# A hybrid layer in another order: z chunks inside the attention rounds, inverted blocks placed by ScalarE

## The reference

```python
qa_l, ka_l, va_l, za_l, g_l, be_l, qb_l, kb_l, vb_l = split_hybrid_projection(a_lat @ w_in, conv_w, ...)
qa_c, ka_c, va_c, za_c, g_c, be_c, qb_c, kb_c, vb_c = split_hybrid_projection(a_ctx @ w_in, conv_w, ...)
o_ctx_a, s_fwd, s_bwd = bidirectional_delta(qa_c, ka_c, va_c, g_c, be_c, zeros, zeros, ctx_out)
o_lat_a, _, _ = bidirectional_delta(qa_l, ka_l, va_l, g_l, be_l, s_fwd, s_bwd, True)
qb_l = apply_axial_rope(qb_l, cos, sin)
kb_l = apply_axial_rope(kb_l, cos, sin)
o_lat_b = latent_attention_blocks(group(qb_l), k_all, v_all)
y = rms_norm(o_lat_a, out_norm) * silu(za_l)
y_lat = concatenate([y, o_lat_b]) @ w_out
```

## Time and profile before

| what | us |
|---|---|
| median of three executions | 2290.75 (2288.51 to 2290.96) |
| the profiled execution, its own time | 2290.72 |
| its span, first to last instruction | 2288.9 |
| TensorE matmul busy | 2220.6 |
| VectorE busy | 1618.4 |
| ScalarE busy | 1156.7 |
| GpSimd busy | 153.3 |

### The profile page before, as it was taken

The page is one execution under the profiler, slowest core; times in us unless marked ns, Lnnn a source line. Parts: engine busy times, 40 slices in busy tenths (PEclk is TensorE's granted clock), DMA queues, the critical chain, the costliest instruction groups (busy, mean ns, idle before and its releaser), DMA issues.

```text
span 2288.9 us, 41418 instructions
## 1 busy us (share of the span) xinstructions
PE 2220.6 (97%) x17332; PEld 2045.3 (89%) x17332; DVE 1618.4 (71%) x2749; ACT 1156.7 (51%) x1937; POOL 153.3 (7%) x142
## 2 busy tenths in 40 slices
PE   7999999999989999999999999999999999999998
PEld 3665889998879999999999989997779999999998
DVE  4399668655977645798557687577988557799654
ACT  3425445443365446756346564345556345957343
POOL 0013000000000000000000000015630000000000
PEclk9999999999999999999999999999999999999999
DMA  8148054555244554415554325562025554514552
GB/s 346 73 183 317 37 221 166 185 186 201 92 166 168 187 186 171 173 57 184 184 182 157 141 93 203 184 221 74 19 94 183 184 184 169 183 55 166 185 184 92
DMA packets 50873, 368.46 MB, mean 161 GB/s; under 512 B 5632, under 2 KB 5888, under 8 KB 6528
## 3 DMA queue, kind: packets, MB, share of 16 engines
q1 hardware_dynamic: 50544, 363.72, 43.2%
q10 hardware_dynamic: 144, 2.10, 0.2%
HBM read 364.75 MB, written 1.05 MB: 160 GB/s over the span
## 4 chain that ended last, share of the span: by engine, by line
PE 81%; DVE 11%; ACT 5%; issue 2%; DMA 0%; SPq 0%; DVEq 0%; POOL 0%; ACTq 0%
PE psum L263 67%; DVE weight_rest L257 2%; PE psum L4508 1%; PE psum L3069 1%; PE psum L4509 1%; ACT weight_parts L221 1%; PE psum L4530 1%; PE psum L3703 1%; PE psum L2719 1%; DVE work L2021 1%; PE psum L4544 1%; DVE work L3533 1%; DVE spare L2509 0%; DVE work L2508 0%; DMA weight_ring<-stream_dram 0%
## 5 line engine op out<-in xcount | busy, mean ns | idle before, releaser
L263 PE MATMUL psum<-input_parts,weight_parts 128*128 128x256 f32 x5184 | 933.0, 283 | 6.0 <-DVE work L1489 1.8
L263 PEld LDWEIGHTS psum<-input_parts,weight_parts 128*128 128x128 f32 x5184 | 801.0, 189 | 11.2 <-issue 5.3
L263 PE MATMUL psum<-input_parts,weight_rest 128*128 128x256 f32 x2592 | 733.6, 283 | 0.0
L257 DVE TENSOR_TENSOR weight_rest<-weight_ring,weight_parts 128x1024 fp32r<-128x1024 f32 x528 | 621.1, 1222 | 151.8 <-ACT weight_parts L221 151.3
L221 ACT ACTIVATE weight_parts<-weight_ring 128x1024 fp32r<-128x1024 f32 x540 | 538.1, 1051 | 128.2 <-PE psum L263 105.6
L263 PEld LDWEIGHTS psum<-input_parts,weight_rest 128*128 128x128 f32 x2592 | 488.9, 189 | 0.0
L263 PE MATMUL psum<-hidden_parts,weight_parts 128*128 128x256 f32 x2496 | 450.7, 283 | 2.6 <-DVE weight_rest L257 1.3
L263 PEld LDWEIGHTS psum<-hidden_parts,weight_parts 128*128 128x128 f32 x2496 | 385.1, 189 | 6.0 <-issue 3.4
L263 PE MATMUL psum<-hidden_parts,weight_rest 128*128 128x256 f32 x1248 | 352.2, 282 | 0.0
L263 PEld LDWEIGHTS psum<-hidden_parts,weight_rest 128*128 128x128 f32 x1248 | 235.0, 188 | 0.0
L1473 ACT ACTIVATE work<-psum 128x256 f32<-128x256 f32 x118 | 45.3, 384 | 352.3 <-PE psum L263 349.9
(11 more groups left out here) (532 smaller groups left out, 2855.4 us busy)
## 6 DMA issues: line engine op xcount, KB each, us to landing
weight_ring<-stream_dram SPq DMA_DIRECT2D x340, 1024.0 KB, 4.8
constants<-constants_dram SPq DMA_DIRECT2D x1, 2304.0 KB, 12.5
work<-s_bc_dram ACTq DMA_DIRECT2D x1, 2048.0 KB, 9.8
work<-ctx_dram SPq DMA_DIRECT2D x1, 1024.0 KB, 5.5
residual<-x_dram SPq DMA_DIRECT2D x1, 1024.0 KB, 7.6
work<-first_dram SPq DMA_DIRECT2D x1, 1024.0 KB, 14.9
out_dram<-residual SPq DMA_DIRECT2D x4, 256.0 KB, 2.1
vectors<-vectors_dram SPq DMA_DIRECT2D x1, 486.5 KB, 11.8
```

Source lines behind the costliest of these rows:

```text
L257: ins = dve.tensor_tensor(self.rest[:, i % RING, cols], self.ring[:, i % RING, cols], self.parts[:, s % SPLITS, cols].bitcast(F32), ALU.su ...
L263: mm = pe.matmul(*args, **kw)
```

## The change

The diff puts the projection into another order: the delta q heads come right behind the k heads, then two v heads, then k, v and q of attention, then the last two v heads. The four z chunks leave the projection: one each is computed in attention rounds 0, 1, 4 and 5, half of it in each of the round's two places for a fill; ScalarE takes them plainly, and one silu over all four stands in the delta stage. Fills stay in rounds 2, 3, 6 and 7, and the projection has sixteen slabs of them instead of eight. VectorE's list of the projection is written anew for this, with three takings inside it. ScalarE gathers the diagonal blocks (`collect`) and puts the inverted ones into their matrices (`place`, in rounds 4 to 7), where GpSimd did; GpSimd keeps the clearing. The attention's probabilities get memory of their own, since their place now still holds the layer's input for z. The core of the diff:

```diff
+        self.attention_work = sb("attention_work", [P, 8 * T2])
...
-FILL_AFTER = (11, 13, 15, 17)
-BESIDE_PROJECTION = 2 * len(FILL_AFTER)
+FILL_AFTER = {9: 2, 11: 2, 13: 4, 15: 4, 17: 4}
+BESIDE_PROJECTION = sum(FILL_AFTER.values())
+LATE_CHUNKS = 4
+LATE_ROUNDS = (0, 1, 4, 5)
+FILL_ROUNDS = (2, 3, 6, 7)
...
-        self.sums_after = {4: (0, 1), 5: (2,), 6: (3, 4), 7: (5, 6), 8: (7,), 9: (8,)}
-        self.lower_after = {8: 0, 9: 1, 11: 2, 13: 3}
+        self.sums_after = {4: (0, 1), 5: (2,), 6: (3,), 11: (4,), 13: (5,), 14: (6,), 15: (7,), 16: (8,)}
+        self.lower_after = {8: 0, 9: 1, 10: 2, 11: 3}
+        self.turns_after = {16: 4, 17: 1}
...
+    def late_silu(self, act):
+
+        act.wait_ge(*self.late_taken[-1])
+        z = self.k.area(H_Z, LATE_CHUNKS * T)
+        act.activation(z, z, ACT.Silu).then_inc(self.late_ready[0], 1)
...
+        self.lower.vector(dve, 2)
+        self.normalize(dve, 4)
+        k.background.take(dve, STRIPS)
+        self.lower.vector(dve, 3)
+        self.normalize(dve, 5)
+        self.blocks.gather(dve)
+        self.normalize(dve, 6)
+        self.blocks.steps(dve, 0, 8)
+        self.normalize(dve, 7)
+        k.background.take(dve, 2 * STRIPS)
+        self.blocks.steps(dve, 8, 15)
+        self.normalize(dve, 8)
+        self.convolve(dve, 10)
+        k.background.take(dve, 3 * STRIPS)
         dve.wait_ge(k.consts_loaded, 16)
         for i in range(5):
             self.rotate(dve, i)
...
         self.convolve(dve, 11)
         self.blocks.steps(dve, 15, EARLY_STEPS)
-        k.background.take(dve, BESIDE_PROJECTION)
...
+            if r in LATE_ROUNDS:
+                self.late_jobs[r] = k.job(k.hyb.late_taken[LATE_ROUNDS.index(r)])
             if r >= 3 and r % 2 == 1:
...
+    def beside(self, pe, r, half):
+
+        if r in LATE_ROUNDS:
+            self.k.hyb.late_half(pe, LATE_ROUNDS.index(r), self.late_jobs[r], half)
+        else:
+            self.k.background.fill(pe, 2)
...
+            if r - 1 in LATE_ROUNDS:
+                k.hyb.take_late(act, LATE_ROUNDS.index(r - 1), self.late_jobs[r - 1])
...
+            if r in (4, 5):
+                self.blocks.place(act, r - 4, 0)
+            if r in (6, 7):
+                self.blocks.place(act, r - 6, 1)
...
-                k.background.take(dve, BESIDE_PROJECTION + 2 * r + 2)
+                k.background.take(dve, BESIDE_PROJECTION + 2 * sum(n < r for n in FILL_ROUNDS))
...
+        k.background.take(dve, BEFORE_DELTA)
...
+                far = self.lc[at, :, :].rearrange("p r (s m) -> p s m r", s=SEQS)
+                for s in range(SEQS):
+                    ins = act.activation(self.b[at, s, :, at], far[:, s], ACT.Identity)
+            else:
+                ins = act.activation(self.a[at, :, at], self.near[at, :, :].rearrange("p s m -> p m s"), ACT.Identity)
```

More of the change, by code:

```diff
@@ L1787, in tensor @@
         front = k.front
+        turned = 0
         for n, (job, (_, tokens, _)) in enumerate(zip(self.jobs, self.chunks)):
@@ L1890, in scalar @@
             else:
-                act.activation(x, job.ap[:, 0:seqs * T], ACT.Silu if kind == "silu" else ACT.Identity)\
-                   .then_inc(self.taken[n][0], 1)
+                act.activation(x, job.ap[:, 0:seqs * T], ACT.Identity).then_inc(self.taken[n][0], 1)
             if 1 <= n <= 4:
                 self.silu(act, n - 1)
-            if n >= 18:
-                self.silu(act, 2 * n - 32)
-                self.silu(act, 2 * n - 31)
             if n == 4:
@@ L1912, in scalar @@
                     self.lower.take_turned(act, m - 1)
-            if n == 14:
+            if n == 13:
                 self.lower.take_turned(act, 3)
+                self.blocks.collect(act)
+            if n == 16:
+                self.lower.tails(act)
+                act.preload_act_table_set("silu_and_others")
+                for i in range(4, 10):
+                    self.silu(act, i)
+        self.silu(act, 10)
+        self.silu(act, 11)
         act.preload_act_table_set(EXP_LN)
@@ L1984, in vector @@
             self.rotate(dve, i)
-        self.convolve(dve, 7)
-        k.background.take(dve, STRIPS)
-        self.lower.vector(dve, 3)
-        for i in range(8, 10):
-            self.convolve(dve, i)
-        self.blocks.gather(dve)
-        self.blocks.steps(dve, 0, 8)
-        self.convolve(dve, 10)
-        self.blocks.steps(dve, 8, 15)
         self.convolve(dve, 11)
         self.blocks.steps(dve, 15, EARLY_STEPS)
-        k.background.take(dve, BESIDE_PROJECTION)
     def gate_values(self, dve):
@@ L2030, in normalize @@
         if 4 <= i < 9:
-            gain = self.k.v("hyb_q_norm" if i < 8 else "hyb_k_norm")
+            gain = self.k.v("hyb_q_norm" if i > 4 else "hyb_k_norm")
         else:
@@ L2113, in tensor @@
                               start=True, stop=True).then_inc(job.full[0], 1)
-                k.background.fill(pe, 2)
+                self.beside(pe, r, 0)
             if r >= 3 and r % 2 == 1:
@@ L2450, in gpsimd @@
             at = self.quarter(q)
[L2451 to L2474 removed]
+            ins = act.activation(self.near[at, :, :], l[at, :, at], ACT.Identity)
+        ins.then_inc(self.gathered[0], 1)
     def quarter(self, q):
@@ L2855, in vector @@
             if first < len(self.steps) - DIRS:
-                k.background.take(dve, BESIDE_PROJECTION + 2 * len(k.attention_rounds) + first + 2)
+                k.background.take(dve, BEFORE_DELTA + first + 2)
         k.weights.split_through(dve, self.next_slab)
@@ L4823, in hyb_columns @@
 def hyb_columns():
-    return np.r_[512:1024, 2064 + hyb_heads(), 2576:2832, 0:512, 1024:2048]
+    return np.r_[512:1024, 0:512, 1024:1280, 2576:2832, 2064 + hyb_heads(), 1280:2048]
 def beside_projection(w, mod):
+    early = len(w) - LATE_CHUNKS // 2
     out, n = [], 0
-    for j in range(len(w)):
+    for j in range(early):
         if j:
             out.append(w[j:j + 1])
-        if 2 * j + 1 in FILL_AFTER:
+        fills = FILL_AFTER.get(2 * j + 1, 0)
+        out.append(mod[n:n + fills])
+        n += fills
+    for r in range(2 * B_PAIRS):
+        if r in FILL_ROUNDS:
             out.append(mod[n:n + 2])
             n += 2
+        elif LATE_ROUNDS.index(r) % 2 == 0:
+            j = early + LATE_ROUNDS.index(r) // 2
+            out.append(w[j:j + 1])
     return np.concatenate(out + [mod[n:]], 0)
```

153 lines of the change are left out of this document (83 added, 70 removed).

## The result

| | before | after |
|---|---|---|
| median, us | 2289.63 (2288.03 to 2290.96, 4 executions) | 2315.37 (2309.49 to 2321.79, 4 executions) |
| ratio | 1 | 1.0113 (95% interval 1.0085 to 1.0142) |
| profiled execution, us | 2290.72 | 2321.79 |
| span, us | 2288.9 | 2320.0 |
| first product of the delta stage | 233.23 | 256.08 |

Slower by 25.7 us, as to sign what was forecast (+14.7), as to size above the range's end of 2311. The profiled execution is the longest of the four; its extra 31.1 us of span fall into 22.85 up to the delta stage, 6.8 from there to a mark 296 us further on (the first table load of ScalarE after 500 us, 529.46 before, 559.09 now) and 1.5 behind that.

What follows compares the result with a forecast made beforehand. TensorE, 97% busy, bounds the kernel, so its waits were summed: 3.7 + 0.9 + 6.0 + 2.6 + 1.1 + clock 1.7 - (0.99 and 0.53) + 0.2 = +14.7 us on 2290.75: 2305.4, range 2297 to 2311.

Steps and rivals of the forecast that it cites:

- wait A: Fill after chunk 15 in the projection: TensorE waits for VectorE's second taking of modulation rows, 3.7 us.
- rotation 4: Before the first attention scores: TensorE waits for VectorE's rotation after head 8 is turned, 0.9 us.
- wait B: Rounds 0 and 1: TensorE waits for first probabilities, behind VectorE's convolution 11 and inversion steps 15 to 22, 6.0 us.
- wait C: Round 2: the second score job waits for probabilities 2 because of its PSUM bank, 2.6 us.
- D, E, F, H: Smaller waits: z-job banks in rounds 1 and 6, output 0's copy, the delta stage's first mask; 5.95 us charged.
- G: End of the attention rounds: the last values product waits for ScalarE's copy, 0.9 us.
- half clock behind A: After the fill's wait behind chunk 15: one fall of the granted clock to 0.50, charged at 1.7 us.
- weight ring: Weight slabs on SP's queue: the same megabytes in another order, so nothing charged.
- the gates: The gates' wait near 80 us, longer because one head's sum left from before it, 0.2 us.
- The rule on GpSimd and VectorE: GpSimd reading SBUF blocks VectorE instructions with two SBUF inputs; 2.1 us handed back to VectorE, not subtracted from the forecast.
- third rival: ScalarE's strided block copies at GpSimd's price, 7.4 us on top: 2309 or 2313; sign: over 1.5 us each; chance 0.08.
- anything behind the delta stage: All behind the delta stage keeps its length; a changed length there would mean something unnamed is at work.

Runs made afterwards that it cites:

- second taking: Changed kernel with VectorE's second taking of modulation rows ahead of inversion steps 0 to 7 instead of behind them: 2311.4 us, ratio 1.0089.
- steps early: Changed kernel with inversion steps 15 to 22 moved from behind convolution 11 to ahead of normalization 8: 2306.9 us, ratio 1.0082.
- five products: Changed kernel with five 128 x 512 products that nobody reads put on TensorE ahead of round 0's turning: 2313.6 us, ratio 1.0111.
- two at a time: Changed kernel with two modulation slabs behind every odd chunk from 5 to 15, and the first two takings earlier: 2302.3 us, ratio 1.0052.
- The three mends: Changed kernel with placing back on GpSimd, two slabs behind odd chunks 5 to 15, and inversion steps 15 to 22 ahead of normalization 8: 2294.0 us, ratio 1.0023.

## Why the prediction was wrong

By its terms, up to the first product of the delta stage in the profiled execution (the pauses of before that fall away, 7.3 us, are the same on both sides):

| term | charged | measured |
|---|---|---|
| wait A | 3.7 | 4.00 |
| rotation 4 | 0.9 | 0.94 |
| wait B | 6.0 | 5.52 |
| wait C, with the half clock ahead of it | 2.6 | 1.30 + 1.86 |
| D, E, F, H | 5.95 | 1.22 + 1.53 + 1.25 + 1.85 = 5.85 |
| G, values behind ScalarE | 0.9 | 1.32 + 2.58 = 3.90 |
| half clock behind A | 1.7 | 5.35 - 3.66 = 1.69 |
| weight ring | 0 | 2.07 + 0.38 = 2.45 |
| half clock behind the ring | 0 | 5.38 - 3.62 = 1.76 |
| half clock at the last values | 0 | 2.97 - 1.95 = 1.02 |
| the gates | 0.2 | 1.87 - 1.74 = 0.13 |

Charged, less 7.3: 14.7. Measured, less 7.3: 23.1, where the trace has 22.85; its projection started 0.28 us earlier than before (43.64 for 43.92), which is the difference.

**What was right.** A, the rotation, B and the sums D to H but for G are within half a microsecond of what was laid end to end from the rows of before; undoing A's and B's causes (second taking, steps) took these waits away, and brought out 1.50 us more at the ring and 1.53 more at C behind them. C itself was nearly right at full clock: 2.83 with the steps early and with five products. "Behind wait B a fall costs nothing" is shown by the five products. That the delta stage's silu and its table loads cost nothing holds: "to mark" is 296.22 with them and 296.23 before. The rule on GpSimd and VectorE stays out of the sum: convolution 10's four operations take 3.11 us now, as the rows without GpSimd said (3.05).

**Step 1 that failed: "ScalarE gets them for nothing as long as its pauses in the rounds hold them".** Two errors in one. The price was read off a row of contiguous elements, 9 us in all, though the only row with this access pattern, GpSimd's, said 16.4; the copies took 16.25, those of 1024 elements 1.98 each, over the 1.5 that was named as the third rival's sign. And a pause that holds the work does not hide it: ScalarE serves in order, and the pieces stood ahead of copies that TensorE needed next. The third rival had the price and the place and got 0.08. The Trainium skill (SBUF — State Buffer, Door 1: The DMA port swizzle) says that SBUF is read in lines of 16 bytes and that each access that crosses to a new line pays; the trace agrees, 1.98 us for a step of 32 elements against 1.05 for runs.

**Step 2: "On SP's queue the slabs are the same megabytes in another order; I charge nothing".** A mean DMA share over a stage says nothing of a burst. The stage around chunk 14 of the kernel after, cut at the fill's start and at the wait (length, TensorE busy, granted clock, DMA share, GB/s), and the row on the slabs of its view of DMA issues (KB each, median us from issue to landing):

```profile
140.00:141.50 1.50, 1.50 (x30) 1.00 0.00 0
141.50:143.76 2.26, 2.26 (x44) 1.00 0.77 290
143.76:145.83 2.07, 0.00 (x1) 1.00 1.00 396
```

```profile
weight_ring<-stream_dram SPq DMA_DIRECT2D x340, 1024.0 KB, 4.8
```

When the fill of four slabs starts, the ring of five is full (the slab of chunks 12 and 13, and these four) and the queue idle; a place comes free only as TensorE goes on to the next slab, a slab takes 4.8 us to land, and the four are used up in 3.66. The queue is then full for the whole wait. Before, two slabs at most stood together; with two at a time the wait does not occur. In six other kernels with this order up to chunk 14 it was 1.82 to 3.45 us.

**Step 3: "I charge one such fall".** Charged 1.7; the layer paid 1.69 + 1.76 + 1.02 that reached the path, and the delta stage's start another 2.9 (5.46 - 2.92, and 0.4 at the group behind it), then some 1.5 at 371.5 (the kernel with placing on GpSimd has such a fall alone between the delta stage and the mark, 297.71 for 296.23). That is 4.4 of the 6.8 us behind the start of the delta stage, the "anything behind the delta stage" that the prediction named as a sign of something it had not seen. Another 0.6 stands in the readout, where TensorE waits 0.93 us for ScalarE in place of 0.24, and the last 1.8 in products that take about 1% longer from 375 us to the mark in this one of the traced executions; the runs do not show why. The falls vary: three of the four executions were 6 to 12 us shorter than the profiled one, with a mean granted clock of 0.991 to 0.994 against 0.990.

The three mends answer the three groups of causes and bring 2315.4 to 2294.0; of what was then left, the longest wait (3.47) was again on a taking in the wrong place. What stays open is which pause is followed by a fall of the clock (below): that chunk 14 lost 1.76 us in the profiled execution was bad luck in part, since the same chunk ran at full clock in four of six other kernels. So the clock's part of one execution's time can be read, but not forecast to a microsecond.

## What to carry to other kernels

Price a moved copy by a row with its own access pattern, whatever engine that row is from, and ask what stands behind it in the new engine's list, not whether that engine has idle time. When fills are regrouped, compare the largest burst that stands together with what the queue brings in that time; a stage's mean share hides it. A wait just behind another wait may cost nothing, and a mend of the first then shows up as the second: look for the next bracket before adding up the savings.

## What the runs showed of the hardware

The granted clock did not follow a pause's length alone. The fill behind 3.47 us of idle time ran at half clock in one run and behind 3.45 at full clock in the next, shown above. Chunk 14 ran at half clock behind 2.07 us in the change, and with placing on GpSimd at full clock behind a longer wait:

```profile
145.96 3.69 PE L263 MATMUL psum<-work,weight_ring 128*128 128x256 f32 x16 [3.30 <-DMA weight_ring<-stream_dram]
```

The waits of 1.33, 2.59 and 1.86 us before the delta stage left the clock alone in the run with five products, while 1.32, 2.58 and 1.85 in the change had it at 0.50 for some ten microseconds. And a pause of 1.58 us at the same instruction of a later layer was followed by half clock in the change and not in the kernel before. First the kernel before, two records:

```profile
345.09 0.48 PE L263 MATMUL psum<-raw_parts,weight_parts 128*128 128x258 f32 x2 [1.58 <-DVE raw_parts L691]
```

and the change:

```profile
371.46 0.75 PE L263 MATMUL psum<-raw_parts,weight_parts 128*128 128x258 f32 x2 [1.58 <-DVE raw_parts L692]
```

ScalarE and GpSimd were equally fast at the same SBUF copies: 4.25 and 4.31 us for the gathering, 16.25 and 16.14 us for the placing. GpSimd's two, from the run with both on GpSimd and the run with placing alone:

```profile
140.87 4.31 POOL L2518 COPY spare<-spare 32x1024 f32<-32x1024 f32 x4 [94.84 <-ACT spare L2416]
```

```profile
220.79 16.14 POOL L2515 COPY work<-spare 32x1024 f32<-32x1024 f32 x8
```
